# Sparse attention loop of a two-layer decoder trunk: value products ahead of the turns of probabilities, copies one place later

## The reference

```python
s_s = jnp.einsum('bqghd,bgqmd->bghqm', qr, k_g).astype(jnp.float32) * scale
p_s = jax.nn.softmax(jnp.where(mask_s, s_s, NEG_INF), axis=-1)
o_s = jnp.einsum('bghqm,bgqmd->bqghd', p_s.astype(v_g.dtype), v_g)
...
s_w = jnp.einsum('bqghd,bkgd->bghqk', qr, kwin).astype(jnp.float32) * scale
p_w = jax.nn.softmax(jnp.where(mask_w, s_w, NEG_INF), axis=-1)
o_w = jnp.einsum('bghqk,bkgd->bqghd', p_w.astype(vwin.dtype), vwin)
return g[..., 0:1] * o_c + g[..., 1:2] * o_s + g[..., 2:3] * o_w
```

## Time and profile before

| | before |
|---|---|
| median of 3 runs | 1326.27 us (1326.1 to 1327.52) |
| the profiled execution | 1325.6 us, of which the span of the profile is 1323.7 us |
| granted PE clock, mean | 0.999 |
| busy share of the span: PE, ACT, DVE, POOL | 99%, 42%, 52%, 15% |
| the loop (PE), first turn to end of last round | 784.03 to 898.83 us from the span's start |
| ACT and DVE busy, 793.52 to 898.83 | 85.1 us and 83.9 us of 105.3 us |

### The profile page before, as it was taken

One profiled execution on the slowest core, in us unless ns is written; L12 is line 12 of the kernel. 1 busy time (PEld: TensorE's weight loads), 2 busy tenths in 40 slices (PEclk: granted clock), 3 DMA queues, 4 the chain that ended last, 5 costly groups with the idle time before them and its releaser, 6 DMA issues.

```text
span 1323.7 us, 17963 instructions
## 1 busy us (share of the span) xinstructions
PE 1313.6 (99%) x6416; PEld 1050.4 (79%) x6416; DVE 692.0 (52%) x1292; ACT 554.7 (42%) x1008; POOL 199.5 (15%) x212
## 2 busy tenths in 40 slices
PE   9999999999999999999999999999999999999998
PEld 7777788888888888888788865568888888888887
DVE  5678886543333333232698778776433333333222
ACT  4436764433333333222274457785333333332222
POOL 2003571221111110100000002112211111110100
PEclk9999999999999999999999999999999999999999
DMA  8332222333333333332244310001333333333311
GB/s 250 82 80 65 65 65 64 96 96 95 95 95 95 95 107 112 106 87 79 80 127 120 95 33 17 1 1 33 98 93 95 96 97 99 100 116 102 104 48 64
DMA packets 206424, 114.11 MB, mean 86 GB/s; under 512 B 5760, under 2 KB 203648, under 8 KB 206240
## 3 DMA queue, kind: packets, MB, share of 16 engines
q1 hardware_dynamic: 205936, 113.03, 29.6%
q0 software_dynamic: 416, 0.35, 0.3%
q10 hardware_dynamic: 16, 0.00, 0.0%
HBM read 111.27 MB, written 2.10 MB: 86 GB/s over the span
## 4 chain that ended last, share of the span: by engine, by line
PE 96%; DVE 2%; issue 1%; ACT 1%; DMA 0%; POOL 0%; SPq 0%; POOLq 0%; DVEq 0%; ACTq 0%
PE acc L734 26%; PE acc L736 26%; PE acc L735 26%; PE acc L1312 3%; PE aux L1299 2%; PE aux L1219 2%; PE acc L1219 1%; PE aux L914 1%; PE acc L1299 1%; PE aux L924 1%; PE acc L1201 1%; PE aux L1180 1%; PE aux L933 0%; PE acc L856 0%; PE acc L865 0%
## 5 line engine op out<-in xcount | busy, mean ns | idle before, releaser
L604 DVE TENSOR_TENSOR w_low<-raw,w_high 128x1024 fp32r<-128x1024 f32 (+2 forms) x184 | 240.3, 1306 | 488.3 <-ACT w_high L585 488.2
L734 PE MATMUL acc<-y_high,w_high 128*128 128x512 f32 x992 | 392.1, 395 | 0.5 <-DVE w_low L596 0.3
L736 PE MATMUL acc<-y_high,w_low 128*128 128x512 f32 x992 | 386.6, 390 | 0.0
L735 PE MATMUL acc<-y_low,w_high 128*128 128x512 f32 x992 | 386.2, 389 | 0.0
L585 ACT ACTIVATE w_high<-raw 128x1024 fp32r<-128x1024 f32 (+2 forms) x185 | 205.0, 1108 | 302.3 <-PE acc L736 296.3
L734 PEld LDWEIGHTS acc<-y_high,w_high 128*128 128x128 f32 x992 | 185.8, 187 | 41.1 <-DVE w_low L596 1.7
L736 PEld LDWEIGHTS acc<-y_high,w_low 128*128 128x128 f32 x992 | 185.7, 187 | 39.9
L735 PEld LDWEIGHTS acc<-y_low,w_high 128*128 128x128 f32 x992 | 185.9, 187 | 38.8 <-issue 0.7
L734 PE MATMUL acc<-ffn_high,w_high 128*128 128x512 f32 (+1 forms) x374 | 141.0, 377 | 0.0
L736 PE MATMUL acc<-ffn_high,w_low 128*128 128x512 f32 (+1 forms) x374 | 140.8, 377 | 0.0
L735 PE MATMUL acc<-ffn_low,w_high 128*128 128x512 f32 (+1 forms) x374 | 140.8, 377 | 0.0
(11 more groups left out here) (348 smaller groups left out, 1663.8 us busy)
## 6 DMA issues: line engine op xcount, KB each, us to landing
raw<-in_l_w_gate_dram SPq DMA_DIRECT2D x44, 512.0 KB, 3.8
raw<-in_l_w_up_dram SPq DMA_DIRECT2D x44, 512.0 KB, 3.8
raw<-in_l_w_down_dram SPq DMA_DIRECT2D x32, 704.0 KB, 4.5
raw<-in_l_w_in_dram SPq DMA_DIRECT2D x43, 512.0 KB, 3.9
raw<-in_l_w_out_dram SPq DMA_DIRECT2D x16, 512.0 KB, 3.6
raw<-in_l_w_in_dram SPq DMA_DIRECT2D x10, 256.0 KB, 3.0
raw<-in_l_cmp_w_k_dram SPq DMA_DIRECT2D x4, 512.0 KB, 3.8
raw<-in_l_cmp_w_v_dram SPq DMA_DIRECT2D x4, 512.0 KB, 3.8
```

Source lines behind the costliest of these rows:

```text
L604: dve.tensor_tensor(dst, src, high.bitcast(F32), ALU.subtract).then_inc(S("split_low"), 1)
L734: pe.matmul(o, ah, bh, start=first, stop=False)
L735: pe.matmul(o, ah, bl, start=False, stop=False)
L736: return pe.matmul(o, al, bh, start=False, stop=last)
```

## The change

In PE's loop, each round's value products now stand right behind the round's scores; the turns of the last round's probabilities and the `sums_turn` come behind them. In `places_of_takes`, the copies of the rounds of 512, 384 and 256 keys come behind one set more (ACT's copy that stood ahead of the first set comes behind set 0); a copy that was behind the last set stays there. The places in rounds 20 to 23 are as they were, and so are all instructions, their number and their operands.

```diff
@@ places_of_takes
     if len(sets) == 4:
         if batch_tiles(sets[0] // 8) == 3:
-            return ((-1, 1) if on_act(takes_in(k - 1)[0]) else (0,)) if act else (1, 3)
-        return (0, 1) if act else (1, 3)
+            return ((0, 2) if on_act(takes_in(k - 1)[0]) else (1,)) if act else (2, 3)
+        return (1, 2) if act else (2, 3)
     if batch_tiles(sets_in(k - 1)[0] // 8) == 1:
         return (5,) if act else (3, 7)
     if batch_tiles(sets[0] // 8) == 1:
         return (0, 3) if act else (4, 7)
-    return (1, 3) if act else (4, 7)
+    return (2, 4) if act else (5, 7)
@@ trunk, PE's loop over the rounds
                     set_scores(n)
                     if n in (5, 7):
                         cmp_sum(n // 2)
+                for b, s in values_in(k):
+                    set_values(b, s)
                 for t in takes_in(k - 1):
                     take_turn(t)
                 for b in ended_in(k - 1):
                     sums_turn(b)
-                for b, s in values_in(k):
-                    set_values(b, s)
                 for q in rows_turned_in(k):
                     rows_turn(q)
```

## The result

The kernel after takes 1337.38 us (median of 4 runs, 1336.91 to 1338.4), the kernel before 1326.6 in the same comparison (4 runs, 1326.1 to 1327.52): ratio 1.0083, 95% interval 1.0071 to 1.0095, so 0.8% slower. The profiled execution of after took 1338.4 us with a span of 1336.6, 12.8 more than the profiled execution of before.

The account below looks back on a forecast made before the run. PE was taken to bound the kernel, holding 96% of the chain. The terms 2.0 + 0.3 + 0.7 + 1.0 + 1.15 + 0.8 + 5.3 made 11.2 us more, so 1337.5 us, range 1331.5 to 1342.

Parts of the forecast that it names:

- The bank waits of rounds 5, 7 and 9: Rounds of 384 keys: PE's value product waits 0.5 us for the bank in rounds 5, 7, 9 and 11, together 2.0.
- Round 13: Scores of 512 keys are longer, so the value product's wait is between 0 and 0.5 us; 0.3 taken.
- round 21: First of the rounds of 128 keys to enter the closed ring of waits: 0.9 us more, half of 1.8.
- The rounds of 128 keys: Rounds 21 to 23: 0.9, then 1.8 each from a ring of waits, and 0.8 for the last maximum; together 5.3 us.
- Rounds 16 to 20: Bank waits of 1.0 us in round 17 and 0.8 in round 20, plus net 1.15 around the rows' and fourth turns.
- PE's waits ahead of `rows_turn`: Rounds 17 to 20: PE waits for ACT's second copy, 0.5 us three times and 0.7 in round 20, together 2.2.
- The wait ahead of the fourth turn: Rounds 16 to 20: PE's wait of 0.21 us for ACT's copy goes, giving 1.05 us back.
- two weight splits: DVE's split in round 10 delays maxima for round 11's scores by 0.6 us; with 0.1 for ACT's in round 8, 0.7.
- The waits go and none come: Rival: copies of the sums keep their distance, PE only loses its 1.05 us of waits: 1325.2 us; chance 0.07.
- Only the short rounds pay: Rival: ACT runs ahead in rounds of 384 to 256 keys, only 5.3 and 0.8 us remain: 1332.4 us; chance 0.12.
- The new switch costs both charges: Rival: PE's value products behind scores pay both switch charges, 4.2 us more: 1341.7 us; chance 0.09.
- costs nothing: Rival: PE's switch from scores to value products is free, 3.2 us less: 1334.3 us; within the forecast's 0.72.

Follow-up runs that it names:

- the rounds up to 15 alone: Kernel after with the whole change kept in rounds 0 to 15 only, old order and places from round 16 on: 1329.46 us, ratio 1.0024.
- the sums early: Kernel after, but ACT copies a batch's sums in the round of its last value product, behind the third set's exponential: 1330.38 us, ratio 1.0032.
- the places alone: Kernel after with PE's old order put back, so only the copies stand one place later: 1330.91 us, ratio 1.0034.
- PE's order alone: Kernel after with the copies at their old places, so only PE's order is new: 1345.16 us, ratio 1.0143.
- the sums later: Kernel after, but ACT copies the sums behind the next round's first exponential instead of ahead of it: 1358.8 us, ratio 1.0248.

## Why the prediction was right

**The mechanism.** The forecast was waits of value products for the one bank, because ACT's copy of the sums stands behind a copy that waits for turns. The chain shows that sequence link by link, and moving that one copy in ACT's list moves the time in both directions, +4.1 and +32.6 against 11. That is shown, not only argued.

**The terms.** The bank waits of rounds 5, 7 and 9 came out at 0.59 each where 0.5 was taken. (The idle time in brackets is 0.52; it is counted from the modelled end of the scores, and a piece that doesn't wait starts 0.07 before that: in before the scores of 807.48 end at 808.29, the next piece starts at 808.22.) The difference is the hand-over from ACT to PE: in round 7 of after the copy of the sums ends at 809.54 in ACT's timeline and the product starts at 809.69, so 0.15, where the sum took the 0.05 between DVE and ACT. Round 13 had 0.39 for 0.3, round 21 0.85 for 0.9; both terms were chosen between two bounds, and that they fit so well is in part luck. The rounds of 128 keys gave 0.85 + 1.83 + 2.65 (without the clock) = 5.33 for 5.3.

Rounds 16 to 20 (net 2.95 predicted: 1.0 + 1.15 + 0.8) gave 2.99, and here two errors cancel, which is luck. PE's waits ahead of `rows_turn` cost 0.37 in each of rounds 17 to 19 and 0.53 in round 20, 1.64 in sum where 2.2 was taken. The wait ahead of the fourth turn gave back 0.14 + 0.07 + 0.17 = 0.38 where 1.05 was taken: the working left out that the turn of the sums would then wait in its place.

**What was mis-sized.** Besides these, the term "two weight splits", 0.7, was almost nothing: round 11 took 6.05 and round 7 5.94, so 0.1. The step that failed took the split's 1.75 us from the earlier trace rows as the price in its new place. The timelines: POOL's of before, then DVE's and POOL's of after:

```profile
821.46 2.26 POOL L2641 TENSOR_TENSOR o_rows<-o_rows,work 128x512 f32<-128x512 f32 x1
```

```profile
824.27 1.22 DVE L604 TENSOR_TENSOR w_low<-raw,w_high 128x1024 fp32r<-128x1024 f32 x1
```

```profile
824.43 2.19 POOL L2641 TENSOR_TENSOR o_rows<-o_rows,work 128x512 f32<-128x512 f32 x1 [0.94 <-DVE work L2433]
```

In before the split at 820.83 ran beside two POOL instructions and took 1.75; in after it started first, POOL's sum came 0.16 behind it, and the split took 1.22. The 0.53 that is missing is nearly all of the 0.6 that was charged. The waits for the bank were 0.09 larger in each of five rounds, and these two errors nearly cancel in the sum.

**The total.** 11.2 was predicted; the rounds give 12.6, of which 1.35 is the fallen clock that no term held. The medians differ by 1337.38 - 1326.6 = 10.8, since the profiled execution of after is 1.0 above its median and that of before 1.0 below its own of that comparison. The mechanism was right; that the median came within 0.2 us of the forecast of 1337.5 is luck, since single terms were off by 0.5 to 0.7.

**The rivals.** "The waits go and none come": the waits ahead of the fourth turn did go and gave back 0.38, but waits for the bank of 7.6 us came. "Only the short rounds pay": the rounds up to 15 alone cost 3.25. "The new switch costs both charges" and "costs nothing": scores 1.49 and product 1.01 in the first chain of after are what they were, and in the run with the sums early PE's new order takes 3.96 and 5.35; so the new order neither costs nor saves a switch.

Two small differences have no term in the sum and nearly cancel: the -0.17 of round 3 and the +0.25 of round 4. The -0.17 is also there with the places alone, and not with PE's order alone, where round 4 has +0.72. At both places the weights of the second pair of scores wait for DVE's maxima: 0.63 us in round 3 of before and 0.46 of after, and 0.59 in round 4 of after, where before has no such wait.

## What to carry to other kernels

Work moved ahead on the engine that bounds a kernel takes with it the distance that hid its neighbours' lists; count, for each thing the moved work waits for, what stands ahead of its release on the other engine, and whether that is itself waiting for what was moved behind. Where a single buffer closes such a ring, move its release in the other engine's list together with the work (here the position of one copy was worth 7 us less or 22 us more than in the kernel after), and judge by the chain, since the busy share of the bound engine stayed at 99% throughout. Where that engine's pieces already follow one another without a hole, as in rounds 5 to 15 here, a new order has only waits to add.

## What the runs showed of the hardware

The granted clock can fall from 1.00 to 0.50 behind waits as short as 1.38 us: in the profile of after it did so behind the second of two such waits, in two other profiles with the same two waits (1.39 each) it stayed at 1.00. In the run with the sums later it fell behind waits of 2.17, 2.17 and 2.24 us and stayed at 1.00 behind waits of 1.96 (801.76) and 2.39 (813.53), so the length of the last wait doesn't decide it alone. Where it fell, what stood behind took 1.35 us longer in the one profile, and 4.7 us in the other. The mean granted clock can't tell whether the other executions of after had the fall too: it is 0.998 in all four of them, but 0.998 or 0.999 in the executions of before. What decides whether it falls was not found.

Of a weight split on DVE (128x1024) and an instruction on POOL that overlap, the one that started second was longer, by nearly the time that the first still ran. Alone the split takes 1.23 us (at 929.50 in before) and POOL's sum 1.28 (at 812.47 in before). In after the split started first and took 1.22; POOL's sum came when 1.06 us of it were left and took 2.19, so 0.91 more. In before POOL was at work when the split started and began its next instruction 0.63 us later; the split took 1.75, so 0.52 more. With the places alone POOL's next instruction began 0.93 us behind the split's start, and the split took 2.05, so 0.82 more. The sum that began behind it, with 1.12 us of the split left, took 2.26 in both, so 0.98 more. So the price of the split in a new place hangs on which of the two engines starts first.
